# Two residuals of a fused two-block kernel: modulation groups, order of sums and splits, handover in halves

## The reference

```python
hx = rmsnorm(x, norm_g[i, 0]) * (1.0 + sc_x) + sh_x          # sc, sh, g: from silu(c) @ w_mod[i] + b_mod[i]
yx = conv_module(hx, *cp)                                    # ends with u @ w_pw2 + b_pw2
x = x + g_x * rmsnorm(yx, norm_g[i, 1])                      # first residual (r0)
fx = rmsnorm(x, norm_g[i, 2]) * (1.0 + scf_x) + shf_x
x = x + gf_x * rmsnorm(swiglu(fx, ffn_w1[i], ffn_w3[i], ffn_w2[i]), norm_g[i, 3])   # second residual (r1)
hx = rmsnorm(x, norm_g[1, 0]) * (1.0 + sc_x) + sh_x          # layer 1, into q, k, v
```

## Time and profile before

| | us |
|---|---|
| median of 3 runs | 1969.12 (1967.93 to 1972.91) |
| span of the profiled execution | 1969.0 |
| PE busy | 1889.2 (96%) |
| DVE busy | 1201.8 (61%) |
| ACT busy | 953.6 (48%) |
| POOL busy | 542.5 (28%) |

### The profile page before, as it was taken

The page is one execution under the profiler, slowest core; times in us unless marked ns, Lnnn a source line. Parts: engine busy times, 40 slices in busy tenths (PEclk is TensorE's granted clock), DMA queues, the critical chain, the costliest instruction groups (busy, mean ns, idle before and its releaser), DMA issues.

```text
span 1969.0 us, 36121 instructions
## 1 busy us (share of the span) xinstructions
PE 1889.2 (96%) x14718; PEld 1668.6 (85%) x14718; DVE 1201.8 (61%) x2440; ACT 953.6 (48%) x1709; POOL 542.5 (28%) x685
## 2 busy tenths in 40 slices
PE   6999999999998989999998999999999999999998
PEld 4855778888886857899987989999999899989997
DVE  4989763233338575655579675685648876567473
ACT  4314532232224477544456474565555556456464
POOL 1320010000001533000021222747373322374736
PEclk9999999999999999899999999999999999999999
DMA  9335442222224254655544444455554544545551
GB/s 358 128 108 206 151 150 96 97 97 97 97 97 171 86 193 175 211 182 182 183 160 175 142 136 160 165 168 172 194 182 152 174 148 133 168 150 178 187 178 59
DMA packets 84548, 307.24 MB, mean 156 GB/s; under 512 B 9376, under 2 KB 10656, under 8 KB 84128
## 3 DMA queue, kind: packets, MB, share of 16 engines
q1 hardware_dynamic: 84384, 304.94, 45.4%
HBM read 303.86 MB, written 1.05 MB: 155 GB/s over the span
## 4 chain that ended last, share of the span: by engine, by line
PE 82%; DVE 10%; ACT 5%; DMA 2%; issue 1%; SPq 0%; POOL 0%; DVEq 0%; ACTq 0%
PE pb L540 18%; PE pb L542 18%; PE pb L541 18%; PE pb L513 7%; PE pb L514 6%; PE pb L519 6%; DVE wlo L1897 2%; DMA raw<-wstream 2%; ACT whi L1237 1%; PE pb L591 1%; DVE Y L2146 1%; PE pb L765 1%; PE pb L924 1%; PE pb L1108 1%; PE pb L1121 1%
## 5 line engine op out<-in xcount | busy, mean ns | idle before, releaser
L540 PE MATMUL pb<-Hh,whi 128*128 128x256 f32 (+1 forms) x2304 | 701.8, 305 | 1.8 <-DVE SM L2480 1.6
L542 PE MATMUL pb<-Hh,wlo 128*128 128x256 f32 (+1 forms) x2304 | 694.6, 301 | 0.0
L541 PE MATMUL pb<-Hl,whi 128*128 128x256 f32 (+1 forms) x2304 | 694.6, 301 | 0.0
L1237 ACT ACTIVATE whi<-raw 128x1024 fp32r<-128x1024 f32 x468 | 489.3, 1054 | 318.1 <-PE pb L542 171.2
L2855 POOL TENSOR_TENSOR wlo<-raw,whi 128x256 fp32r<-128x256 f32 x576 | 434.9, 790 | 734.9 <-ACT whi L1237 733.9
L1897 DVE TENSOR_TENSOR wlo<-raw,whi 128x1024 fp32r<-128x1024 f32 x324 | 421.2, 1305 | 344.1 <-ACT whi L1237 343.7
L540 PEld LDWEIGHTS pb<-Hh,whi 128*128 128x128 f32 x2304 | 441.9, 192 | 22.9 <-DVE SM L2480 2.5
L541 PEld LDWEIGHTS pb<-Hl,whi 128*128 128x128 f32 x2304 | 442.2, 192 | 15.0
L542 PEld LDWEIGHTS pb<-Hh,wlo 128*128 128x128 f32 x2304 | 442.0, 192 | 15.0
L513 PE MATMUL pb<-Hh,whi 128*128 128x256 f32 (+1 forms) x528 | 161.2, 327 | 4.6 <-ACT Hh L1311 3.2
L514 PE MATMUL pb<-Hh,wlo 128*128 128x256 f32 (+1 forms) x528 | 158.8, 322 | 0.0
(11 more groups left out here) (333 smaller groups left out, 2952.6 us busy)
## 6 DMA issues: line engine op xcount, KB each, us to landing
raw<-wstream SPq DMA_DIRECT2D x572, 512.0 KB, 3.5
X<-xin SPq DMA_DIRECT2D x2, 1024.0 KB, 7.7
out<-X SPq DMA_DIRECT2D x8, 128.0 KB, 1.8
CON<-consts SPq DMA_DIRECT2D x1, 926.0 KB, 8.6
VEC<-vecs SPq DMA_DIRECT2D x1, 662.0 KB, 9.5
CON<-consts SPq DMA_DIRECT2D x1, 147.0 KB, 3.8
VEC<-vecs SPq DMA_DIRECT2D x1, 88.0 KB, 2.0
```

The source lines that it names most:

```text
L540: e.matmul(dst, hi, xh, start=k == 0, stop=False)
L541: e.matmul(dst, hi, xl, start=False, stop=False)
L542: i = e.matmul(dst, lo, xh, start=False, stop=k == kt - 1)
L1237: e.activation(whi[:, s % NPIECE, :], raw[:, p % NRAW, :], ACT.Copy).then_inc(sig("act_hi", ("hi", p)), 1)
```

## The change

Six edits, in the first layer and around it:
1. `MODS`: set F gets a fourth group, taken from set A, which keeps two. F has eight bites, A four. The stream's order follows.
2. `sums3` takes `first` and `then` in the place of `step`. r0: the running sum of y, no bite, the other running sums, one bite, tiles 6 and 7 without a bite between, two bites. r1: two bites, running sums, tiles 6 and 7, two bites. Nothing is left of the two bites that stood around r1's first `widen`.
3. The FFN's bites stand after the k steps 2 to 6 (before: 2 to 4). The squares of y in the last part's down tiles are summed one tile earlier, that of tile 5 behind the last down tile and ahead of `sums3`.
4. In the last part, for down tiles 6 and 7, ACT's splits stand behind the squares, and DVE's behind the addition and, for both tiles, behind the last product `xz(7)`.
5. `mt` signals each half of a tile, and ACT's `modulated` waits for each half by itself. This holds for every norm of 512 columns, the first one (`n0`) too.
6. `ready()` in r1 stands ahead of the second reciprocal, and both residuals have the order `mt(0)`, `rt(1)`, `low(0)`, `rt(2)`.

```diff
--- before.py
+++ after.py
@@ -33,7 +33,7 @@
 FIRST = 4
 
 
-MODS = {"S0": (0, 2, 2), "S1": (1, 2, 2), "C": (4, 4, 1), "N": (8, 2, 1), "F": (10, 3, 1), "A": (13, 3, 1),
+MODS = {"S0": (0, 2, 2), "S1": (1, 2, 2), "C": (4, 4, 1), "N": (8, 2, 1), "F": (10, 4, 1), "A": (14, 2, 1),
         "T0": (16, 4, 1), "T1": (20, 2, 1), "G": (22, 2, 1)}
 MOST = 4
 
@@ -633,12 +633,10 @@
                 i.then_inc(sig("pe_stat", point), 1)
 
 
-            def sums3(S, R, step):
+            def sums3(S, R, first, then):
                 if S == "y0":
                     sums_y(S, R, None)
-                else:
-                    step()
-                    sums_y(S, R, 5)
+                bite(first[0])
                 b = slots.at(("stat", S))
                 for key, o in ((S + "b", 128), (S + "c", 256)):
                     w.wait_ge(*on("acc", key))
@@ -646,8 +644,8 @@
                         i = e.matmul(b[32 * c:32 * c + 32, o:o + 128], con("mean", 0, 32),
                                      slots.at(("acc", key))[:, c * 128:(c + 1) * 128], start=False, stop=False)
                     i.then_inc(sig("pe_stat", ("asum", key)), 1)
+                bite(first[1])
                 for k in (6, 7):
-                    step()
                     for key, o in ((S, 0), (S + "b", 128), (S + "c", 256)):
                         w.wait_ge(*on("sq", key, k))
                         for c in range(4):
@@ -655,7 +653,7 @@
                                          slots.at(("sq", key, k))[:, c * 128:(c + 1) * 128], start=False,
                                          stop=o == 256 and k == 7)
                         i.then_inc(sig("pe_stat", ("sums", key) if k == 7 else ("xsum", key, k)), 1)
-                step()
+                bite(then)
 
 
             def sums_y(S, R, k):
@@ -723,7 +721,7 @@
             acc_sums("x0", 512, ("xm",))
             bite(1)
             mod_tr()
-            widen("x0", 512, ("mt", "n0", 7))
+            widen("x0", 512, ("mt", "n0", 7, 1))
             bite(1)
 
 
@@ -806,16 +804,16 @@
             for m in range(FIRST, 8):
                 lin([("pw2", m)], 8, H2, 512, hx("cn"))
             feed("F")
-            sums3("y0", "r0", lambda: bite(1))
+            sums3("y0", "r0", (0, 1), 2)
             widen("y0", 512, ("rdone", "r0", 7), idle=2)
-            widen("r0", 512, ("mt", "n1", 7))
+            widen("r0", 512, ("mt", "n1", 7, 1))
 
             def ffn(l, parts, n, S, Yk):
                 src = H2 if n == 512 else H1
                 j0 = 0
                 for pi, cnt in enumerate(parts):
                     ups = [("up", l, j0 + j, s) for j in range(cnt) for s in range(2)]
-                    lin_first(ups[:FIRST], 8, src, n, hh(S), hx(S), idle=5 if l == pi == 0 else 0, between=lambda k: bite(1) if l == pi == 0 and k in (2, 3, 4) else None)
+                    lin_first(ups[:FIRST], 8, src, n, hh(S), hx(S), idle=5 if l == pi == 0 else 0, between=lambda k: bite(1) if l == pi == 0 and 1 < k < 7 else None)
                     for u in ups[FIRST:]:
                         lin([u], 8, src, n, hx(S))
                         if pi == 0 and u is ups[FIRST]:
@@ -826,7 +824,7 @@
                     for m in range(FIRST, 8):
                         lin([downs[m]], *dargs)
                         if l == 0 and pi == len(parts) - 1:
-                            for k in {4: (0, 1), 5: (2,), 6: (3,), 7: (4,)}[m]:
+                            for k in {4: (0, 1, 2), 5: (3,), 6: (4,), 7: (5,)}[m]:
                                 sums_y("y1", "r1", k)
                     j0 += cnt
                 if l:
@@ -834,12 +832,10 @@
 
             ffn(0, FFN0, 512, "n1", "y1")
             feed("A")
-            bite(1)
-            sums3("y1", "r1", lambda: bite(1))
+            sums3("y1", "r1", (2, 0), 2)
             widen("y1", 512, ("rdone", "r1", 7))
-            bite(1)
             mod_tr()
-            widen("r1", 512, ("mt", "n2", 7))
+            widen("r1", 512, ("mt", "n2", 7, 1))
 
 
             def head_sums(key, n):
@@ -951,7 +947,7 @@
             residual("r2", "y2", T)
             bite(2)
             x_sums("r2", T, (3,))
-            widen("r2", T, ("mt", "n3", 7))
+            widen("r2", T, ("mt", "n3", 7, 0))
             ffn(1, FFN1, T, "n3", "y3")
             residual("r3", "y3", T)
 
@@ -1306,8 +1302,8 @@
             def modulated(S, l, shift, segs, k):
                 t = slots.at(("mt", S, k))
                 w.wait_ge(*on("mod", l, 2 * shift + k // 4))
-                w.wait_ge(*on("mt", S, k))
                 for s in range(segs):
+                    w.wait_ge(*on("mt", S, k, s))
                     i = e.activation(Hh[:, k * 512 + s * T:k * 512 + (s + 1) * T], t[:, s * T:(s + 1) * T], ACT.Identity,
                                      bias=mvec(l, shift, s, k))
                 i.then_inc(sig("act_x", ("xh", S, k)), 1)
@@ -1447,7 +1443,8 @@
                         preload(ACT.Sqrt)
                     for m in range(8):
                         y = Y[:, m * 512:m * 512 + n]
-                        hi_to(("down", l, pi, m))
+                        if l or pi < len(parts) - 1 or m < 6:
+                            hi_to(("down", l, pi, m))
                         if pi == 0:
                             w.wait_ge(*on("lin", "down", l, pi, m))
                             e.activation(y, slots.at(("lin", "down", l, pi, m))[:, 0:n], ACT.Copy).then_inc(
@@ -1460,6 +1457,8 @@
                                 t = buf(stage, "sq", ("sq", Yk, m), ("sums", Yk) if m == 7 else ("xsum", Yk, m))
                                 e.activation(t, y, ACT.Square).then_inc(sig("act_sq", ("sq", Yk, m)), 1)
                                 z_square(stage, Yk, m, 3)
+                                if m > 5:
+                                    hi_to(("down", l, pi, m))
                     j0 += cnt
                     if pi < len(parts) - 1:
                         hi_to(("down", l, pi, 7), 5)
@@ -1968,9 +1967,9 @@
                     if R != "x0":
                         w.wait_ge(*on("x", R, k))
                     for s in range(segs):
-                        i = e.scalar_tensor_tensor(out=t[:, s * T:(s + 1) * T], in0=X[:, s, k, :], scalar=MA[:, l, slot, s, k:k + 1],
-                                                   in1=r[:, s * T:(s + 1) * T], op0=ALU.mult, op1=ALU.mult)
-                    i.then_inc(sig("dve_x", ("mt", S, k)), 1)
+                        e.scalar_tensor_tensor(out=t[:, s * T:(s + 1) * T], in0=X[:, s, k, :], scalar=MA[:, l, slot, s, k:k + 1],
+                                               in1=r[:, s * T:(s + 1) * T], op0=ALU.mult, op1=ALU.mult).then_inc(
+                            sig("dve_x", ("mt", S, k, s)), 1)
                     if k == 0 and R != "x0":
                         low(0)
                     if k > (0 if R == "x0" else 1) and (k != 4 or R != "x0"):
@@ -2052,6 +2051,8 @@
                 step(e.tensor_tensor(XM[:, :], XM[:, :], q, ALU.add))
                 after()
                 step(e.tensor_scalar(q, XM[:, :], 0.0, None, ALU.max), ("mean2", R))
+                if ready:
+                    ready()
                 rec4(R, 512)
 
                 def rt(k, segs=(0, 1)):
@@ -2070,10 +2071,10 @@
                     w.wait_ge(*on("spread", R))
                     w.wait_ge(*on("x", R, k))
                     for s in range(2):
-                        i = e.scalar_tensor_tensor(out=t[:, s * T:(s + 1) * T], in0=X[:, s, k, :],
-                                                   scalar=MA[:, l1, slot1, s, k:k + 1],
-                                                   in1=slots.at(("spread", R))[:, s * T:(s + 1) * T], op0=ALU.mult, op1=ALU.mult)
-                    i.then_inc(sig("dve_x", ("mt", N, k)), 1)
+                        e.scalar_tensor_tensor(out=t[:, s * T:(s + 1) * T], in0=X[:, s, k, :],
+                                               scalar=MA[:, l1, slot1, s, k:k + 1],
+                                               in1=slots.at(("spread", R))[:, s * T:(s + 1) * T], op0=ALU.mult,
+                                               op1=ALU.mult).then_inc(sig("dve_x", ("mt", N, k, s)), 1)
 
                 def low(k):
                     t = slots.at(("mt", N, k))
@@ -2088,20 +2089,15 @@
                 w.wait_ge(*on("rt", R, 0))
                 e.tensor_tensor(X[:, 0:2, 0, :], X[:, 0:2, 0, :], two(slots.at(("rt", R, 0))), ALU.add).then_inc(
                     sig("dve_x", ("x", R, 0)), 1)
-                if ready:
-                    rt(1)
-                    rt(2)
-                    ready()
                 mt(0)
-                if not ready:
-                    rt(1)
-                    low(0)
-                    rt(2)
+                rt(1)
+                low(0)
+                rt(2)
                 for k in range(1, 8):
                     mt(k)
                     if k + 2 < 8:
                         rt(k + 2, (0,))
-                    if k > 1 or ready:
```

(5 more changed lines are left out.)

## The result

The changed kernel takes 1978.49 us (median of 8 runs, 1974.7 to 1982.79), beside 1969.42 for the kernel before (8 runs, 1966.23 to 1972.91). The ratio is 1.0042, 95% interval 1.003 to 1.0053, so about +8.3 us (the medians themselves lie 9.1 apart). The forecast was 1973.0 with a range of 1969.2 to 1976.2: the sign was right, the time lies above the range. The profiled execution took 1980.9 us, 2.4 more than the median; its span, 1979.1, is set against the 1969.0 of before.

What follows compares the result with a forecast made beforehand. PE, busy 96% of 1969.0 us, was taken as the bound, with holes only in r0 and r1. Terms -0.4 - 1.1 + 2.44 + 3.0 = +3.9, plus 0.1 from span to median, gave 1973.0, range 1969.2 to 1976.2.

Steps and rivals of the forecast that it cites:

- First norm, -0.4: First norm: the handover in halves brings `xh` up to 0.45 us earlier; taken as -0.4, bounds -0.45 and 0.
- r0, -1.1: Residual after `pw2`: no bite between sums gains 0.95, `low(0)` held by POOL again; -1.1 us, bounds -0.95 and -2.1.
- Two bites in the FFN, +2.44: First four FFN tiles: two more bites at 1.22 us each, hidden by nothing; +2.44, bounds 2.0 and 2.5.
- Rival 3: FFN: five bites make the fifth tile late, 1974.5, or fill DVE-made holes, 1972; chance 0.08 together.
- r1, +3.0: Residual after the first block's FFN: late split, early `ready()` and DVE-bound k tiles outweigh earlier sums; +3.0 us, bounds -0.5 and +3.5.
- The eighth lands near 622.3: r1: split ends 617.4, then 2.6, 1.3 and 1.0 us until A's eighth piece lands; the fourth bite waits 3.2.
- rival 2: r1: PE idles before the fourth bite and its clock falls to half; +2.5 over the forecast, 1975.5 us; chance 0.27.
- The k tiles: r1, after the first product: DVE bounds the two k tiles; r0's order costs +0.67 us, less 0.2 by halves.
- Rival 1: r1: group A arrives in time, so r1 gives -0.5 and the sum is -0.6, 1968.5 us; chance 0.15.

Runs made afterwards that it cites:

- e7: Kernel before with the handover in halves alone (each half of a tile signalled and awaited singly); 1968.11 us, ratio 1.0001.
- e11: Kernel before with the regrouping alone: F eight bites, five between the FFN's k steps, A four; 1973.19 us, ratio 1.0008 to the kernel before.
- e1: Changed kernel with the splits of the last down tiles back at their old place, ahead of squares and products; 1971.99 us, ratio 1.0011 to the kernel before.
- e2: Changed kernel with `ready()` moved to just ahead of `mt(0)`, the split staying late; 1973.95 us, ratio 1.0023 to the kernel before.
- e9: Kernel before with the late split alone: splits behind squares and products in the last two down tiles; 1977.54 us, ratio 1.0031.
- e10: Kernel before with `ready()` ahead of the second reciprocal and r0's order of tile work in r1, A keeping six bites; 1976.54 us, ratio 1.0027.
- e8: Changed kernel with the pieces behind A requested only once A's last piece has landed; 1976.12 us, ratio 1.0028 to the kernel before.
- e4: Changed kernel with eleven PE dummies between the third and fourth bite, where PE would idle; 1975.07 us, ratio 1.0028 to the kernel before.
- e3: Changed kernel with the splits at their old place and `ready()` just ahead of `mt(0)`; 1969.64 us, ratio 0.9999 to the kernel before.
- e5: e3 with two of F's bites in place of four of the five dummies before the FFN, three left in it; 1965.08 us, ratio 0.998.

## Why the prediction came out as it did

**First norm, -0.4: wrong.** The trace of e7 has nothing of it (14.32 beside 14.15), and no time can tell 0.4. The step "ACT goes from its last tile to splits and an eviction that PE awaits" is right, but PE's own matmuls (L519) then end last; the 0.34 that ACT now waits for PE is the lost gain.

**r0, -1.1: right.** -0.85 up to the first product and -1.05 at the end of the second k step; the hold of `low(0)` was met again, as I had taken it. The Trainium skill (GPSIMD Engine Reference, section 8) was the reason to expect it: it says that GpSimd contends with DVE instructions that have two SBUF inputs. The trace agrees: DVE's pair takes 1.92 starting ahead of POOL and 1.85 starting behind it. POOL's addition is stretched only when it starts second (1.47 in the place of 1.28).

**Two bites in the FFN, +2.44: right.** +2.45 in the profile, +1.6 in e11, whose interval (-1.0 to +4.1) holds both. Rival 3 is out: L591's five groups at regular distance, no late fifth tile.

**r1, +3.0: the step that failed.** It measured +6.6, beyond its upper bound of 3.5. The mechanism was the right one (split, seventh buffer, eighth piece, fourth bite, `ready()`), and e1, e2, e9 and e10 confirm its links. Two sizes were off: the landing of the eighth piece, and the clock, which the forecast had left at full speed.
- "The eighth lands near 622.3", 4.9 behind the end of the split. It was 6.2 (617.83 to 624.06). I had added 2.6 for the seventh piece, 1.3 for the eighth at the best rate of a window, and 1.0; I had no term for a rate that dips (262 GB/s here, 156 in e8), nor for what e8's hold took off (0.7 to 0.9, cause open). The split itself came 0.3 sooner than I had reckoned, so 1.1 of the surplus is this. The term that everything hung on had a single size with no range of its own; from the end of the split to the bite the late-split runs have 4.95 (e9) to 6.4.
- The clock. I gave it 0.27 as rival 2 and priced it at +2.5; it fell, and cost 2.5 up to the first product (e4). I set too much by r1's waits of before, which had left the clock at 1.00. They were short in PE's timeline:

```profile
618.67 1.07 PE L591 MATMUL pb<-raw,csz 128*32 128x512 f32 x8 [0.74 <-DMA raw<-wstream]
621.76 1.07 PE L591 MATMUL pb<-raw,csz 128*32 128x512 f32 x8 [1.37 <-DMA raw<-wstream]
```

The row that bore on it was that of the earlier trace rows, where the bite after an idle time of 2.66 had run at half clock, and the wait that I had computed myself, 3.2, was longer than that; it came to 5.12. By that row the fall was the likelier case. The Trainium skill (TensorE: Matmul & The Clock Gate, "Why this matters for your kernels") names this danger, and the trace agrees with it (5.12 without work, then 0.50).

Together: 5.4 from the sums of y to the first product, where 2.5 was predicted: 1.1 for the landing, 0.1 from landing to bite, 2.5 for the clock, less 0.8 because the way from bite to first product at full clock takes 4.2 (e4) and not 5.0. The k tiles give +1.1 for +0.47: 20.0 from the first product to the low-half matmuls, 19.3 in e4 (627.43 to 646.74), so 0.7 of it is the clock again, in the second spread, for which DVE was idle 0.81. e1, with the same order and the spread at full clock, has 19.3 as well. With this the clock cost 3.2, near the 3.4 between the medians.

**The rivals.** Rival 1, A in time, is what e1 is: with the split at its old place the wait is 0.4. Its r1 term of -0.5 is met (-0.4). Its sum of -0.6 is not: e1 has +1.2 in the trace and +2.2 in time (-0.6 to +4.9), since the sum took r0 at its best (-2.1, where -1.05 came) and -0.45 for the first norm. e3, at -0.2, has `ready()` late and is another kernel. Rival 2, the clock, came true, on top of a lateness larger than computed; its sum, 1975.5, lacks what the landing added and has r0's and the first norm's gains in it. The sum of the upper bounds (0 for the first norm, -0.95 for r0, +2.5 for the bites, +3.5 for r1, +2.5 for the clock: +7.55) gives 1976.7, still below the time: the landing needed a bound of its own.

**Open.** Why the DMA rate dips with only two pieces under way, why e9's eighth piece comes sooner than e8's, and how much of e8's 2.4 in the median comes from the hold: the profile has 0.9 for it. Falls of the clock come at various places elsewhere in both kernels, and differ from run to run; single differences of 2 us between kernels that were not measured beside each other are not to be built on.

## What to carry to other kernels

Before an operation is moved on an engine that frees ring buffers, follow the freed buffer to the transfer it starts and to the first instruction that needs those bytes; a split of 1.2 us held back by 5 us cost 6. Work for which an engine waits should not stand ahead of work that could go on (here `ready()` ahead of the second reciprocal), unless it is sure to be there. The fourth bite ahead of the first spread looks like the same fault, since e2's spread still waits behind it, but no run moved it. Fillers pay where PE runs dummies anyway (e5), and cost their full time where it is busy (e11).

## What was unexpected in the hardware

- From the release of the seventh piece's buffer to the use of the eighth it is 4.95 to 6.4 us with more requests behind it (e9, e2, e4, the changed kernel), and 5.5 with two pieces alone (e8). 1 MB at the 418 GB/s of the earlier trace rows would be 2.5, so half of the time or more is not transfer at full rate.
- Eleven dummies, 5.02 us in all, during a wait for data that they cannot shorten, took 2.5 us off the chain behind it (e4).
- DVE's pair is stretched by POOL's addition whichever starts first (from 0.87 to 1.85 or 1.92); POOL's addition only when it starts second (from 1.28 to 1.47).
- In e3 the clock also fell while PE was at work for part of each k step and DVE set the pace:

```profile
628.00:632.00 4.00, 2.40 (x6) 1.11 (x6) 4.00 (x11) 1.81 (x4) 2.56 (x2) 0.80 0.02 8
632.00:636.00 4.00, 3.71 (x9) 2.90 (x10) 4.00 (x11) 1.43 (x4) 2.15 (x2) 0.50 0.00 0
```

The last columns are clock, DMA share and GB/s. DVE (third) is busy throughout, and no longer wait of DVE shows there.
